# Two plain units of the FFN instead of three in a one-core decoder step, with the second pair's preparation in another order

## What is computed

```python
    x = x + gt1 * (merged @ w_out)
    h2 = rms_norm(x, g2) * (1 + sc2) + sh2
    x = x + gt2 * (jnp.square(jax.nn.relu(h2 @ w_up)) @ w_down)
...
    y_prompt = rms_norm(xp, final_g)
    y_sample = rms_norm(xs, final_g)
```

## Time and profile before

| | us |
|---|---|
| median of three runs | 1299.65 |
| the profiled execution | 1299.35 |
| its span | 1297.6 |
| PE busy | 1273.4 |
| DVE busy | 812.8 |
| ACT busy | 577.2 |
| POOL busy | 183.9 |

### The profile page before, as it was taken

How to read it: one execution, slowest core, us unless ns; L and a number is a source line. 1 busy time by engine, 2 the same in 40 slices (tenths; PEclk the granted TensorE clock), 3 DMA queues, 4 the chain that set the end, 5 groups by cost and what they waited for, 6 DMA issues and landing times.

```text
span 1297.6 us, 24740 instructions
## 1 busy us (share of the span) xinstructions
PE 1273.4 (98%) x10221; PEld 1246.0 (96%) x10221; DVE 812.8 (63%) x1221; ACT 577.2 (44%) x998; POOL 183.9 (14%) x182
## 2 busy tenths in 40 slices
PE   6999999999999999999999999999999999999997
PEld 5999999999998999999999999999999999999996
DVE  7611446664334655447798877677678975688874
ACT  5412324444344533336865555555563434334252
POOL 2000100000000122222333333232310000000021
PEclk9999999999999999999999999999999999999999
DMA  9998422222222543545345553544498666776533
GB/s 314 319 289 280 146 66 67 66 80 82 71 67 75 176 128 111 152 124 153 100 125 174 174 165 125 166 132 142 148 340 260 225 202 220 213 240 195 183 126 101
DMA packets 239596, 211.59 MB, mean 163 GB/s; under 512 B 17185, under 2 KB 220837, under 8 KB 234605
## 3 DMA queue, kind: packets, MB, share of 16 engines
q1 hardware_dynamic: 238620, 209.66, 51.1%
q10 hardware_dynamic: 865, 0.36, 0.1%
HBM read 161.97 MB, written 49.04 MB: 163 GB/s over the span
## 4 chain that ended last, share of the span: by engine, by line
PE 91%; DVE 2%; SPq 2%; DMA 1%; ACT 1%; issue 1%; POOL 1%; DVEq 0%; POOLq 0%; ACTq 0%
PE psum L580 29%; PE psum L581 28%; PE psum L582 28%; PE psum L638 2%; PE psum L804 1%; PE psum L792 1%; PE psum L781 1%; DMA ada_p<-in_w_ada_dram 1%; SPq L2206 1%; POOL st L2132 1%; DMA ff_scratch<-st 1%; SPq L2173 1%; DVE b_lo L1829 1%; DVE xl L1792 0%; PE psum L936 0%
## 5 line engine op out<-in xcount | busy, mean ns | idle before, releaser
L580 PE MATMUL psum<-xh,b_hi 128*128 128x264 f32 x908 | 257.2, 283 | 2.2 <-DVE b_lo L1829 1.9
L582 PE MATMUL psum<-xh,b_lo 128*128 128x264 f32 x908 | 257.7, 284 | 0.0
L581 PE MATMUL psum<-xl,b_hi 128*128 128x264 f32 x908 | 256.3, 282 | 0.0
L580 PE MATMUL psum<-dh,e_hi 128*128 128x264 f32 x896 | 254.9, 285 | 0.0
L581 PE MATMUL psum<-dl,e_hi 128*128 128x264 f32 x896 | 253.9, 283 | 0.0
L582 PE MATMUL psum<-dh,e_lo 128*128 128x264 f32 x896 | 253.7, 283 | 0.0
L580 PE MATMUL psum<-h_hi,w_hi 128*128 128x384 f32 (+1 forms) x624 | 207.8, 333 | 1.5 <-issue 1.5
L581 PE MATMUL psum<-h_lo,w_hi 128*128 128x384 f32 (+1 forms) x624 | 201.5, 323 | 0.0
L582 PE MATMUL psum<-h_hi,w_lo 128*128 128x384 f32 (+1 forms) x624 | 201.3, 323 | 0.0
L580 PEld LDWEIGHTS psum<-xh,b_hi 128*128 128x128 f32 x908 | 170.4, 188 | 3.0 <-DVE b_lo L1829 2.5
L581 PEld LDWEIGHTS psum<-xl,b_hi 128*128 128x128 f32 x908 | 170.5, 188 | 0.0
(11 more groups left out here) (315 smaller groups left out, 2418.1 us busy)
## 6 DMA issues: line engine op xcount, KB each, us to landing
down_raw<-in_w_down_dram SPq DMA_DIRECT2D x72, 512.0 KB, 5.5
dr<-ff_scratch SPq DMA_DIRECT2D x28, 1056.0 KB, 8.1
up_raw<-in_w_up_dram SPq DMA_DIRECT2D x76, 256.0 KB, 3.6
ff_scratch<-st SPq DMA_DIRECT2D x64, 264.0 KB, 3.3
ada_p<-in_w_ada_dram SPq DMA_DIRECT2D x8, 2048.0 KB, 9.9
ff_scratch<-st SPq DMA_DIRECT2D x32, 396.0 KB, 3.7
w_raw<-in_w_in_dram SPq DMA_DIRECT2D x22, 512.0 KB, 4.9
gates_scratch<-g_out SPq DMA_DIRECT2D x16, 528.0 KB, 3.2
```

What stands on the lines that cost most here:

```text
L580: mm(out, whi, rhi, start=first, stop=False)
L581: mm(out, whi, rlo, start=False, stop=False)
L582: return mm(out, wlo, rhi, start=False, stop=last)
```

## The change

PLAIN becomes 2. The order is now plain 0, plain 1, units 2 and 3 for both pairs, unit 0 for the second pair, unit 4, unit 1 for the second pair, and the rest for both. There are 120 up steps, and step 8 is the first that reads the second pair. In the second pair X12 and X22 are shifted by DVE (a new "shift", four tensor_scalar instructions each) and not by ACT. The tables put the halves in the order of their first use. The two plain units use different slots of `st` and `st_12` (`lies`), and SP waits for the earlier store before it counts the next one. The wait for the sample bias table shares a semaphore with the sample caches. `Y_AT` puts y 6 and y 7 after the same step and y 8 one step earlier.

```diff
@@ -65,11 +65,11 @@
 
-PLAIN = 3
+PLAIN = 2
 
 UNITS = [("plain", c, (0,)) for c in range(PLAIN)] + [("up", c, (0, 1)) for c in range(PLAIN, 8)]
 for c in range(PLAIN):
-    UNITS.insert(PLAIN + 1 + 2 * c, ("up", c, (1,)))
+    UNITS.insert(PLAIN + 2 + 2 * c, ("up", c, (1,)))
 UNITS += [("up", c, (0, 1)) for c in range(8, 16)]
@@ -148,6 +148,12 @@
 
+def lies(v):
+
+    kind, _, ts = UNITS[v]
+    return slice(v % 2, v % 2 + 1) if kind == "plain" else slice(ts[0], ts[-1] + 1)
+
+
 def stored(v):
@@ -155,7 +161,7 @@
 Y = [(tok, 1, r) for tok in range(2) for r in range(3)] + [(tok, 0, r) for tok in range(2) for r in range(3)]
-Y_AT = [len(TURNS) - 1 - k for k in (10, 9, 8, 7, 6, 5, 3, 2, 1)]
+Y_AT = [len(TURNS) - 1 - k for k in (10, 9, 8, 7, 6, 5, 3, 3, 2)]
 
@@ -187,19 +193,21 @@
 H2_T = [(tok, x) for tok in range(2) for x in (T1, T3, T2, T4)]
-H2_H = [(0, x) for x in (X11, X12, X21, X22, T1, T2, T3, T4)] + [(1, x) for x in (X11, T1, X22, T2, T3, X21, T4)]
+H2_H = [(0, x) for x in (X11, X12, X21, X22, T1, T2)] + [(1, X11), (1, T1), (1, T2), (0, T3), (1, X22), (1, T3), (1, X21), (0, T4), (1, T4)]
+
+H2_S = [(0, X11), (0, X12), (0, X22), (0, X21), (1, X11), (1, X21)]
+H2_V = [(1, X12), (1, X22)]
 
 H2_DVE = {2: (("mul", 0, X12), ("mul", 0, X22)), 3: (("mul", 0, X21),), 4: (("sum", 0, T1), ("sum", 0, T3)),
           5: (("sum", 0, T2), ("low", 0, X11)), 6: (("low", 0, X12), ("sum", 0, T4)), 7: (("low", 0, X21), ("low", 0, X22))}
-F2_DVE = {0: (("low", 0, T1),), 1: (("low", 0, T2),), 2: (("low", 0, T3),), 3: (("mul", 1, X11), ("mul", 1, X12)),
-          4: (("mul", 1, X22), ("mul", 1, X21), ("samples", 1, None)), 5: (("low", 0, T4),), 6: (("sum", 1, T1),), 7: (("sum", 1, T3), ("sum", 1, T2)),
-          8: (("low", 1, X11),), 9: (("low", 1, T1),), 10: (("low", 1, X22),), 11: (("sum", 1, T4), ("low", 1, T2)), 12: (("low", 1, T3),),
-          13: (("low", 1, X21),), 14: (("low", 1, T4),)}
+F2_DVE = {0: (("low", 0, T1),), 1: (("low", 0, T2),), 2: (("mul", 1, X11), ("mul", 1, X12)), 3: (("shift", 1, X12), ("mul", 1, X22)),
+          4: (("shift", 1, X22), ("mul", 1, X21)), 5: (("samples", 1, None), ("sum", 1, T1), ("low", 1, X11)), 6: (("sum", 1, T3), ("sum", 1, T2)),
+          7: (("low", 1, T1),), 8: (("sum", 1, T4), ("low", 1, T2)), 9: (("low", 0, T3),), 10: (("low", 1, X22),), 11: (("low", 1, T3),),
+          12: (("low", 1, X21),), 13: (("low", 0, T4), ("low", 1, T4))}
 H2_ACT = {2: (("shift", 0, X11),), 3: (("shift", 0, X12), ("shift", 0, X22)), 4: (("shift", 0, X21), ("high", 0, X11)),
           5: (("high", 0, X12), ("high", 0, X21)), 6: (("high", 0, X22),), 7: (("high", 0, T1),)}
-F2_ACT = {0: (("high", 0, T2),), 1: (("high", 0, T3),), 2: (("high", 0, T4),), 3: (("shift", 1, X11),), 4: (("shift", 1, X12),), 5: (("shift", 1, X22),),
-          6: (("shift", 1, X21),), 7: (("high", 1, X11),), 8: (("high", 1, T1),), 9: (("high", 1, X22),), 10: (("high", 1, T2),), 11: (("high", 1, T3),),
-          12: (("high", 1, X21),), 13: (("high", 1, T4),)}
+F2_ACT = {0: (("high", 0, T2),), 3: (("shift", 1, X11),), 4: (("high", 1, X11),), 6: (("shift", 1, X21), ("high", 1, T1)), 8: (("high", 1, T2),),
+          9: (("high", 0, T3), ("high", 1, X22)), 10: (("high", 1, T3),), 11: (("high", 1, X21),), 12: (("high", 0, T4), ("high", 1, T4))}
 
...
@@ -697,7 +706,7 @@
                     if hf == 0:
-                        pe.wait_ge(kvc_in, 32)
+                        pe.wait_ge(kvc_in, 48)
                     for q in range(4):
@@ -980,13 +989,13 @@
                     last.then_inc(ready[bank], 1)
-                if e in Y_AT:
-                    y = Y_AT.index(e)
-                    if y == 0:
-                        pe.wait_ge(x2_done, 1)
-                    if y == 6:
-                        copied(("f", N_STEPS - 1, 0))
-                    turn_back(y, 4 + 2 * (y % 2))
+                for y in range(9):
+                    if e == Y_AT[y]:
+                        if y == 0:
+                            pe.wait_ge(x2_done, 1)
+                        if y == 6:
+                            copied(("f", N_STEPS - 1, 0))
+                        turn_back(y, 4 + 2 * (y % 2))
                 if e == len(TURNS) - 2:
@@ -1288,8 +1297,10 @@
                 else:
-                    if x in (X11, X12, X21, X22):
-                        act.wait_ge(n2_raw, H2_X.index((tok, x)) + 1)
+                    if (tok, x) in H2_V:
+                        act.wait_ge(n2_vec, H2_V.index((tok, x)) + 1)
+                    elif x in (X11, X12, X21, X22):
+                        act.wait_ge(n2_raw, H2_S.index((tok, x)) + 1)
                     else:
@@ -1384,11 +1395,10 @@
                     bank, _ = turn["f", n, 0]
-                    c, d = ((st[:, X11, 0, :], st_12[:, 0, :]), (st[:, X21, 0, :], st[:, X22, 0, :]))[i // 2]
-                    for k in ((1,), (2, 0))[i // 2]:
-                        wait(act, st_sent[k], stored(v))
-                    if i == 1:
-                        wait(act, st_sent[0], stored(v))
+                    w = v % 2
+                    c, d = ((st[:, X11, w, :], st_12[:, w, :]), (st[:, X21, w, :], st[:, X22, w, :]))[i // 2]
+                    for k in ((1, 0), (2, 0))[i // 2]:
+                        wait(act, st_sent[k], stored(v - 1) if v else 0)
                     fn(c, psum[:, bank, 0:HB], ACT.Relu)
...
@@ -1639,7 +1650,7 @@
                         tt(ks_lo[:, NB * WIN:SK], z[:, KZ, TP:T], f(ks_hi[:, NB * WIN:SK]), ALU.subtract).then_inc(ks_done, 1)
-                        dve.wait_ge(bs_in, 16)
+                        dve.wait_ge(kvc_in, 48)
                     if i in (14, 16):
@@ -1777,9 +1788,18 @@
                     tt(r[x][:, :, 0:w], x1[:, j:j + 4, c0:c0 + w], R2[tok][:, HB * n:HB * n + w].unsqueeze(1).to_broadcast([P, 4, w]), ALU.mult).then_inc(n2_mul, 1)
+                elif what == "shift":
+                    dve.wait_ge(n2_mul, H2_X.index((tok, x)) + 1)
+                    for k in range(4):
+                        j, raw_x = k + (4 if x == X22 else 0), r[x][:, k, 0:HB - TS]
+                        last = ts_(raw_x, raw_x, gain2[:, j, 0:1], mod[:, 3 * DK + j, 0:1], ALU.mult, ALU.add)
+                    last.then_inc(n2_vec, 1)
                 elif what == "sum":
-                    needs = {T1: X12, T3: X22, T2: X22, T4: X21}[x]
-                    dve.wait_ge(n2_raw, H2_X.index((tok, needs)) + 1)
+                    for needs in {T1: (X11, X12), T3: (X22, X12), T2: (X22,), T4: (X21,)}[x]:
+                        if (tok, needs) in H2_V:
+                            dve.wait_ge(n2_vec, H2_V.index((tok, needs)) + 1)
+                        else:
+                            dve.wait_ge(n2_raw, H2_S.index((tok, needs)) + 1)
                     if tok:
@@ -2066,7 +2086,7 @@
                 freed(("ss", 1, t))
-            pool.wait_ge(kvc_in, 32)
+            pool.wait_ge(kvc_in, 48)
             ch.step(cp(vs_hi[:, :, :], vc[:, :, :]))
...
@@ -2245,7 +2265,7 @@
             sp.dma_start(vc[:, :, :], a["cache_v"][0].rearrange("b w h d -> w b (h d)")).then_inc(kvc_in, 16)
-            sp.dma_start(bias_s[:, :, :], a["alibi_sample"]).then_inc(bs_in, 16)
+            sp.dma_start(bias_s[:, :, :], a["alibi_sample"]).then_inc(kvc_in, 16)
             load_unit(7)
@@ -2349,11 +2369,12 @@
                 kind, c, ts = UNITS[v]
-                sl = slice(ts[0], ts[-1] + 1)
+                if 0 < v <= PLAIN:
+                    sp.wait_ge(st_sent[part], stored(v))
                 sp.wait_ge(t_done, 4 * v + (2 if part == 0 and kind == "plain" else 1 if part == 0 else part + 2))
                 x0, x1_ = ((3, 5), (0, 3), (5, 7))[part]
-                for tok in ts:
-                    sp.dma_start(ff_d[c // 8, x0:x1_, :, tok, c % 8, :].rearrange("k p c -> p k c"), st[:, x0:x1_, tok, :]).then_inc(st_sent[part], 16)
+                for tok, w in zip(ts, range(lies(v).start, lies(v).stop)):
+                    sp.dma_start(ff_d[c // 8, x0:x1_, :, tok, c % 8, :].rearrange("k p c -> p k c"), st[:, x0:x1_, w, :]).then_inc(st_sent[part], 16)
 
```

16 lines of the change are left out of this document (9 added, 7 removed).

## The result

The changed kernel has a median of **1306.15 us** (five runs, 1304.22 to 1307.98) against 1299.65 of the kernel before (five runs, 1297.87 to 1299.98). The ratio is 1.0057, 95% interval 1.0047 to 1.0068: slower by over 0.2%, as forecast, but by 6.5 us where 2.95 were forecast, and above the whole range of the forecast (1298.5 to 1305.6). The profiled execution took 1305.82 us, 1.9 more than its span. Its mean granted clock, 0.994 of full speed, is lower than the 0.997 before, and of the five runs the fastest (1304.22) has the highest, 0.997, and the two slowest the lowest, 0.993.

What follows compares the result with a forecast made beforehand. TensorE, busy for 98% of the span, was taken as the bound; -1.45 (matmuls) + 5.0 (gaps) - 0.6 (end) = +2.95 us, moving the median from 1299.65 to 1302.6 us, range 1298.5 to 1305.6.

Steps and rivals of the forecast that it cites:

- Matmuls, -1.45: First pair: one plain unit becomes Strassen, 12 matmuls fewer at 0.121 us each, -1.45 us with nothing hiding it.
- The deadline and the first stop: Second pair's first product moves from step 12 to 8; T1 ready at 648.8, wanted at 645.5, PE waits 3.3 us.
- The anchor, 631.7: Step 7's weight split, the last point where DVE must wait for PE; DVE's queue is added up from 631.7.
- The queue's own 13.6 us: DVE's own work from step 7's split to the end of T1's low part: 4.2 + 7.0 + 1.3 + 1.1 us.
- The surcharge of 3.4: Ahead of T1, POOL's seven sums for the two plain units slow DVE by 3.4 us.
- So the gaps add up to 8.0 us: Steps 9 to 14: PE's waits for T1 and T4 total 8.0 us where there were 3.0, +5.0 us.
- Banks and the down steps keep their order: Banks and down steps keep their order; no time was added for them.
- The old 3.0 does not come on top; stores and the joint semaphore cost nothing: Old 3.0 us of PE waits vanish as DVE catches up; stores (bounds 0 and 1 us) and shared semaphore cost nothing.
- The end, -0.6: Last product: no block stands in front of DVE's final add, -0.6 us, between all given back and 1.3 gained.
- Covered: Rival: POOL's sums do not slow DVE as before, so 3.4 and 0.57 go; 1298.6 us, chance 0.20.
- faster: Rival at step 9: new order of halves keeps DVE ahead, no gap old or new; 1294.6 us, chance 0.08.
- Full lock: Rival: each POOL sum costs DVE its whole length, 5.4 instead of 3.4, wide one 1.54; 1305.6 us, chance 0.15.

Runs made afterwards that it cites:

- e11: Changed kernel with GpSimd filling T1 to T4 of the two plain units' results with zeros instead of summing: 1301.49 us, ratio 1.0018.
- e10: Changed kernel with e2's buffer order and extra overwritten matmuls ahead of TensorE's waits, 30 at step 9 and 22 at step 14: 1302.79 us, ratio 1.0033.
- e2: Changed kernel with the first three down-weight buffers taken in the order 1, 0, 2 instead of 0, 2, 1: 1304.95 us, ratio 1.0049.
- e4: Kernel before with only the change's new Y_AT and its loops: 1297.80 us, ratio 0.9993.
- e12: Changed kernel with e2's buffer order and 30 extra overwritten matmuls ahead of the wait of step 9 only: 1303.42 us, ratio 1.0033.
- e6: Changed kernel with the second pair's two shifts moved back from VectorE to ScalarE: 1306.76 us, ratio 1.0057.
- e7: Changed kernel with VectorE's low part of the second pair's T1 made two operations earlier: 1305.72 us, ratio 1.0046.

## Why the forecast was half right

The direction, the first stop and its cause came as forecast. Two steps failed: the price of a stop of TensorE, and the down steps that were to keep their order.

**Matmuls, -1.45.** Right. The distance of 0.12 us is the same wherever the clock is at 1.00.

**The deadline and the first stop.** Right, with a small miss. The anchor, 631.7, was met: 630.17 with a start 1.6 earlier. The queue's own 13.6 us were 14.4 (e11); part of the difference is that each shift takes 0.31 and not 0.27, and the samples 1.6 with their waits and not 1.3. The surcharge of 3.4 was 3.4. T1 was ready 17.8 us behind the anchor instead of 17.0. From there to T4 the queue needs 19.6 us (e10) where 19.2 were forecast; the wide sum, beside the last two low parts, cost 1.1 and not 0.57 (3.54 us for two that take 2.42). These together are **+1.2**: the up stretch of e10, in which apart from the extra matmuls only this differs from the forecast, is 4.7 us longer than before, against 3.55.

**"So the gaps add up to 8.0 us".** This is the step that failed. It priced a stop of TensorE by its length and let TensorE go on at the pace of the earlier trace rows behind it. In the FFN of the kernel before no stop was longer than 1.6 us, and the clock was 1.00 around all of them. But far ahead of it the same trace has a stop as long as the one forecast, from 30.57 to 33.82 us, and the clock was at half behind it (TensorE's timeline, then the stretch behind the stop):

```profile
33.82 3.29 PE L638 MATMUL psum<-ada_p,c_pad 128*32 128x128 f32 x64 [2.96 <-DMA ada_p<-in_w_ada_dram]
34.00:36.00 2.00, 2.00 (x44) 1.84 (x43) 1.30 (x2) 0.00 (x0) 0.00 (x0) 0.50 1.10 348
```

So the term at nothing could have been given a bound. In the changed kernel's profile the same place has a stop of 3.0 us and a clock of 1.00, which would have made it a bound and not a value. Measured, the low clock makes the up stretch **1.6 to 2.0 us** longer (342.0 in e2 and 342.4 in the changed kernel against 340.4 in e10). In the changed kernel this is about 1.0 by holding VectorE up in the middle of its backlog (20.6 us from T1 to T4 against 19.6) and about 1.2 by ten slow matmuls at its end.

**"Banks and the down steps keep their order."** This step failed too; it put the down steps at nothing. Nothing in their order changes, but 72 blocks end in other buffers than 76, and the order of three buffers had been fitted to 76. The first down load went out 12.1 us ahead of the first down matmul (944.02 to 956.1), where it had been 16.4 (934.70 to 951.1), and TensorE waited for one of the next. With what hangs on it this is **1.7 us** (e2).

**The old 3.0 does not come on top; stores and the joint semaphore cost nothing.** Right: no wait for `b_lo` or for a store stands among TensorE's waits, and the FFN starts within the scatter of 613.0 to 615.9.

**The end, -0.6.** -0.5 (e4). The last product now waits for TensorE alone, against the earlier trace rows; VectorE's timeline of the changed kernel:

```profile
1290.96 0.49 DVE L1907 SCALAR_TENSOR_TENSOR x<-psum,mod,x 128x264 f32<-128x264 f32 x1
1292.87 0.49 DVE L1907 SCALAR_TENSOR_TENSOR x<-psum,mod,x 128x264 f32<-128x264 f32 x1 [1.42 <-PE psum L591]
```

**Sum.** Behind the start of the FFN the kernel is 8.0 us longer in its profile, where 2.95 were forecast: +1.2 from VectorE's queue, +1.6 to 2.0 from the clock, +1.7 from the down load, and 0.1 from the end. The medians differ by 6.5, the ratio says 6.1 to 8.8. e10, without the two mechanisms that the forecast did not have, is at 1302.79, and 1302.6 was forecast for a kernel that has only the others. That they lie so close is partly luck: the kernel before was at 1298.75 in e10's comparison, so e10 is 4.0 us slower, which is the forecast 2.95 and most of the 1.2 from VectorE's queue.

**The rivals.** Covered and faster fell with the first stop. *Full lock* gave nearly the measured time, 1305.6, and for the wrong reason: e11 puts the seven narrow sums at 3.4 us, not 5.4.

## What to carry to other kernels

A stop of the engine that bounds a kernel is not priced by its length alone. Behind stops of 3 to 7.5 us in the FFN TensorE lost another 1.5 to 2.8 us at half speed here, behind stops of 2.4 us sometimes as much and sometimes nothing, and it shows as busy while it does; so the granted clock has to be read beside the waits. Look for such a place in the whole trace, not only in the part that the change touches. If a later wait is set by another engine, most of that loss is hidden there: the slow matmuls behind step 9 cost 2.3 us in e2, and without them e12's up stretch is 0.9 shorter. Where a change alters how often a ring of buffers is used, look at everything that was fitted to where the ring ended. And when a bundle of edits loses, try its parts without the one that moves the deadline: here that gave the fastest version.

## What was not expected of the hardware

- The same stop of 4.2 us was followed by 13, 22 or 27 matmuls at the low clock in three profiles, and a stop of 2.4 us by 15 or 16 (e2, e12) or by none (e6, e11).
- Stops of 1.9, 0.9 and 2.2 us between 644.16 and 652.03 were followed by the low clock as one long stop was (e7).
- Single-source shifts of VectorE, 0.31 us for 232 columns when alone, took 0.57 each on average beside GpSimd's sums (2.35 for four against 1.33), while GpSimd's fills of the same size, 0.32 us each, slowed none of the operations beside them in e11.
